# Routing matrices of every third batch made from two one-pass products, with GpSimd making part of the columns

## The reference, cut to what matters

```
e = (take_along_axis(i1, ci // 16) * 128 + take_along_axis(i2, ci % 16))
g = softmax(sc)                       # 16 shares for each of 8 heads
ue, ve = u[e], v[e]
hid = einsum('thkd,td->thk', ue, xb)
a = gelu(hid) * g
out = einsum('thk,thkd->td', a, ve)
```

## Time and profile before

| | |
|---|---|
| median of 3 runs | 3039.03 us (3038.13 to 3039.24) |
| span of the profiled execution | 3036.8 us |
| TensorE busy | 3010.5 us |
| VectorE, ScalarE, GpSimd busy | 1840.3, 1147.8, 1919.7 us |
| stage of the routing matrices | some 2242 to 2465 us |

### The profile page before, as it was taken

One profiled execution on the slowest core, in us unless ns is written; L12 is line 12 of the kernel. 1 busy time (PEld: TensorE's weight loads), 2 busy tenths in 40 slices (PEclk: granted clock), 3 DMA queues, 4 the chain that ended last, 5 costly groups with the idle time before them and its releaser, 6 DMA issues.

```text
span 3036.8 us, 42976 instructions
## 1 busy us (share of the span) xinstructions
PE 3010.5 (99%) x15307; PEld 2554.4 (84%) x15307; DVE 1840.3 (61%) x3382; ACT 1147.8 (38%) x2083; POOL 1919.7 (63%) x1812
## 2 busy tenths in 40 slices
PE   8999999999999999999999999999999999999999
PEld 7877888888668888888777888999999998888887
DVE  7675544316865442250673236888868859877785
ACT  3466222103652221120554212444367753333333
POOL 7423766677337666776433576798975576766763
PEclk9999999999999999999999999999999999999999
DMA  7211222223212222222112223699989999999995
GB/s 240 70 43 42 92 97 98 97 96 104 77 45 102 99 97 96 97 104 97 70 56 77 77 91 114 231 330 313 334 301 329 329 363 382 379 362 362 359 368 193
DMA packets 175167, 547.67 MB, mean 180 GB/s; under 512 B 13667, under 2 KB 67076, under 8 KB 155140
## 3 DMA queue, kind: packets, MB, share of 16 engines
q1 hardware_dynamic: 117348, 338.81, 32.5%
q0 software_dynamic: 39168, 142.62, 12.4%
q10 hardware_dynamic: 18464, 63.70, 5.7%
HBM read 487.55 MB, written 57.40 MB: 179 GB/s over the span
## 4 chain that ended last, share of the span: by engine, by line
PE 94%; ACT 2%; DVE 2%; POOL 1%; issue 1%; ACTq 0%; DMA 0%; DVEq 0%; POOLq 0%
PE banks L194 83%; PE banks L2974 2%; PE banks L2290 1%; PE banks L2251 1%; POOL weights_split L3552 1%; PE banks L1151 1%; PE banks L2269 1%; PE banks L2895 1%; PE banks L1807 1%; PE banks L1845 0%; PE banks L1220 0%; PE banks L1823 0%; PE banks L1210 0%; PE banks L1241 0%; DVE memory L3234 0%
## 5 line engine op out<-in xcount | busy, mean ns | idle before, releaser
L194 PE MATMUL banks<-memory,weights_split 128*128 128x512 f32 (+1 forms) x9456 | 2043.1, 373 | 9.6 <-DVE memory L578 8.3
L194 PEld LDWEIGHTS banks<-memory,weights_split 128*128 128x128 f32 x9456 | 1693.0, 188 | 279.1 <-issue 33.0
L3717 POOL TENSOR_SCALAR weights_split<-weights_raw 128x512 fp32r<-128x512 f32 x576 | 374.2, 659 | 748.9 <-issue 372.0
L3722 POOL TENSOR_TENSOR weights_split<-weights_raw,weights_split 128x512 fp32r<-128x512 f32 x576 | 767.6, 1344 | 0.2
L3552 POOL TENSOR_TENSOR weights_split<-weights_raw,weights_split 128x512 fp32r<-128x512 f32 x384 | 506.9, 1344 | 275.3 <-ACT weights_split L3351 272.9
L194 PE MATMUL banks<-weights_split,memory 128*128 128x512 f32 (+1 forms) x2880 | 646.4, 386 | 0.0
L194 PEld LDWEIGHTS banks<-weights_split,memory 128*128 128x128 f32 x2880 | 533.7, 188 | 108.9 <-issue 1.0
L3351 ACT ACTIVATE weights_split<-weights_raw 128x1024 fp32r<-128x1024 f32 x256 | 268.6, 1051 | 38.6 <-DMA weights_raw<-in_weights 20.7
L3054 DVE CUSTOM_DVE_ANT_0 memory<-memory,banks 128x1024 f32<-128x1024 f32 x144 | 174.2, 1213 | 71.4 <-DMA memory<-in_peer_u,memory 68.9
L712 DVE TENSOR_TENSOR banks<-banks,memory 128x512 f32<-128x512 f32 x88 | 61.3, 699 | 231.9 <-PE banks L194 231.8
L3546 POOL DMA_INDIRECT memory<-in_peer_v,memory x128 | 160.4, 1253 | 42.0 <-issue 25.9
(11 more groups left out here) (309 smaller groups left out, 2683.5 us busy)
## 6 DMA issues: line engine op xcount, KB each, us to landing
weights_raw<-in_weights SPq DMA_DIRECT2D x143, 1024.0 KB
weights_raw<-in_weights SPq DMA_DIRECT2D x257, 512.0 KB
routing<-memory ACTq DMA_DIRECT2D x12, 2048.0 KB
hidden<-memory ACTq DMA_DIRECT2D x62, 384.0 KB
memory<-hidden SPq DMA_DIRECT2D x31, 768.0 KB
memory<-routing SPq DMA_DIRECT2D x30, 768.0 KB
window_rows<-memory ACTq DMA_DIRECT2D x1, 3064.0 KB, 26.5
chunk_rows<-memory ACTq DMA_DIRECT2D x1, 2556.0 KB, 12.3
```

The source lines that it names most:

```text
L194: last = k.nc.tensor.matmul(out, left[a], right[b], start=start and n == 0, stop=stop and n == 2, skip_group_check=True)
L3717: k.nc.gpsimd.tensor_scalar(cut(high, n * PIECE, PIECE), cut(raw, n * PIECE, PIECE), 1.0, 1.0, ALU.mult, ALU.mult).then_inc(k.high_made, 1)
L3722: k.nc.gpsimd.tensor_tensor(cut(low, n * PIECE, PIECE), cut(raw, n * PIECE, PIECE), cut(high, n * PIECE, PIECE).bitcast(F32), ALU.subtract ...
```

## The change

For every third batch (g % 3 = 2) the shares no longer scale the rows. The share is split in two parts of type F32R, `share_high` (ScalarE, rounded) and `share_low` (VectorE, what is left). VectorE's `one_hot` writes such a batch as F32R, and `weigh_columns` scales its columns with the high part, in place of `weigh_rows`. GpSimd makes the columns of the lower part in `lower_columns(g)`: one instruction for each token compares the key numbers 0 to 127 with the choice's column and multiplies with the low share. TensorE then makes two one-pass products for each token, with the same rows, summed in PSUM, and writes each token's matrix contiguously; `copy_matrix` reads such a bank in the other order. The shares of these batches alone are copied to PSUM. Several semaphores are merged or renamed. The other two batches in three are as before.

```diff
+    with k.scope(at=8 * KB):
+        share_both, first_columns, second_columns = (k.take(512, F32R) for _ in range(3))
+        share_high, share_low = cut(share_both, 0, P), cut(share_both, P, P)
+        columns_low = [first_columns, second_columns]
+    with k.scope(at=exact_at):
+        exact_hots = [k.take(2 * BATCH * P, F32R) for _ in range(DEPTH)]
...
+    def exact_number(g):
+        return g // 3
...
-                pe.wait_ge(weighted, sum(not by_scalar(n) for n in range(g + 1)))
+                pe.wait_ge(weighted, exact_number(g) + 1)
+                pe.wait_ge(columns_lowered, BATCH * (exact_number(g) + 1))
...
             for t in range(BATCH):
-                last = mm(by_key[:, t, :], cut(hots[g % DEPTH], t * P, P), cut(hots[g % DEPTH], (BATCH + t) * P, P),
-                          start=True, stop=True, skip_group_check=True)
+                if by_scalar(g):
+                    last = mm(by_key[:, t, :], cut(hots[g % DEPTH], t * P, P), cut(hots[g % DEPTH], (BATCH + t) * P, P),
+                              start=True, stop=True, skip_group_check=True)
+                    continue
+                rows = cut(exact_hots[g % DEPTH], t * P, P)
+                out = cut(score_banks[g % 2].memory, t * P, P)
+                mm(out, rows, cut(exact_hots[g % DEPTH], (BATCH + t) * P, P), start=True, stop=False,
+                   skip_group_check=True)
+                last = mm(out, rows, cut(columns_low[exact_number(g) % 2], t * P, P), start=False, stop=True,
+                          skip_group_check=True)
...
-        def weigh_rows(g):
-            rows = cut(hots[g % DEPTH], 0, BATCH * P).rearrange("p (t n) -> p t n", t=BATCH)
+        def weigh_columns(g):
+            columns = cut(exact_hots[g % DEPTH], BATCH * P, BATCH * P).rearrange("p (t n) -> p t n", t=BATCH)
             dve.wait_ge(hot, g + 1)
-            v.tensor_tensor(rows, rows, cut(shares, g * BATCH, BATCH).unsqueeze(2).broadcast_to(three),
+            v.tensor_tensor(columns, columns.bitcast(F32),
+                            cut(shares, exact_number(g) * BATCH, BATCH).unsqueeze(2).broadcast_to(three),
                             ALU.mult).then_inc(weighted, 1)
...
-        dve.wait_ge(iota_placed, 2)
+        dve.wait_ge(matrix_inputs, 3)
+        v.tensor_tensor(share_low.rearrange("p (c n) -> p c n", n=BATCH), exact_shares,
+                        share_high.rearrange("p (c n) -> p c n", n=BATCH).bitcast(F32),
+                        ALU.subtract).then_inc(matrix_inputs, 1)
...
                          score_banks[g % 2].memory.rearrange("p (n t) -> p n t", t=BATCH),
+                         score_banks[g % 2].memory.rearrange(
+                             "p (n t) -> p n t" if by_scalar(g) else "p (t n) -> p n t", t=BATCH),
...
-                        a.activation(shares, cut(turned, 2 * DENSE, DENSE), ACT.Copy).then_inc(iota_placed, 1)
+                        a.activation(share_high.rearrange("p (c n) -> p c n", n=BATCH), exact_shares,
+                                     ACT.Copy).then_inc(matrix_inputs, 1)
+                        act.wait_ge(matrix_inputs, 2)
+                        a.activation(shares, share_high.bitcast(F32), ACT.Copy).then_inc(matrix_inputs, 1)
...
+        def lower_columns(g):
+            number = exact_number(g)
+            if number == 0:
+                pool.wait_ge(matrix_inputs, 4)
+            if number >= 2:
+                pool.wait_ge(made, g - 5)
+            k.hold(pool)
+            for t in range(BATCH):
+                k.nc.gpsimd.tensor_scalar(cut(columns_low[number % 2], t * P, P), k.const("iota"),
+                                          cut(turned, DENSE + g * BATCH + t, 1),
+                                          cut(share_low, number * BATCH + t, 1).bitcast(F32), ALU.is_equal,
+                                          ALU.mult).then_inc(columns_lowered, 1)
+
         for unit in range(UNITS):
+            for g in matrix_after.get(unit - 3, ()):
+                if not by_scalar(g):
+                    lower_columns(g)
             if not by_vector(unit):
                 pool.wait_ge(unit_high, unit + 1)
```

More of the change, by code:

```diff
@@ L2669, in expert_layer @@
         hots = [k.take(2 * BATCH * P) for _ in range(DEPTH)]
+        exact_at = k.pointer - DEPTH * 8 * BATCH * P
         expert_f, expert, share_of, hid, applied = (k.take(P) for _ in range(5))
@@ L2748, in expert_layer @@
     (keys_in, normalised, scored, copied, order, exp_in, exp_out, chosen_ready, turned_up, emptied, activated, hot,
-     weighted, made, matrix_copied, iota_placed, multiplied, high_made, ready, used, out_filled, gain_in, result_summed,
+     weighted, columns_lowered, made, matrix_copied, matrix_inputs, multiplied, high_made, ready, used, out_filled, gain_in, result_summed,
      result_sized, result_rooted, result_inverted, result_made, unit_begun, unit_high, residual_turned, residual_kept,
@@ L2752, in expert_layer @@
          "keys_in", "normalised", "scored", "scores_copied", "order", "to_exp", "exped", "chosen", "turned", "emptied",
-         "activated", "hot", "weighted", "made", "matrix_copied", "iota_placed", "multiplied", "high_made", "ready",
+         "activated", "hot", "weighted", "columns_lowered", "made", "matrix_copied", "matrix_inputs", "multiplied", "high_made", "ready",
          "used", "out_filled", "gain_in", "result_summed", "result_sized", "result_rooted", "result_inverted",
@@ L2758, in expert_layer @@
         k.lasting("experts_last_" + s) for s in ("weighed", "made", "scaled", "half_out"))
-    (ones_placed, picked_summed, masks_made, numbered, spread_copied, numbers_made, picked_turned,
+    (ones_placed, picked_summed, picking_made, spread_copied, numbers_made, picked_turned,
      factors_made, factors_placed, factors_turned, picked_weighed) = (k.lasting("experts_" + s) for s in (
-         "ones_placed", "picked_summed", "masks_made", "numbered", "spread_copied", "numbers_made", "picked_turned",
+         "ones_placed", "picked_summed", "picking_made", "spread_copied", "numbers_made", "picked_turned",
          "factors_made", "factors_placed", "factors_turned", "picked_weighed"))
@@ L2781, in expert_layer @@
     largest, inverse = cut(iota, 0, PEER_HEADS), cut(best_cols, 0, PEER_HEADS)
-    shares = cut(scratch_bank.memory, 0, DENSE)
+    shares = cut(scratch_bank.memory, 0, P)
+    exact_shares = cut(turned, 2 * DENSE, DENSE).rearrange("p (c n) -> p c n", n=3 * BATCH)[:, :, 2 * BATCH:3 * BATCH]
     index4 = index_f.rearrange("p (s h r) -> p h s r", h=PEER_HEADS, s=2)
@@ L2937, in spread_numbers @@
         def spread_numbers():
-            pe.wait_ge(masks_made, 3)
-            pe.wait_ge(numbered, 1)
+            pe.wait_ge(picking_made, 4)
             mm(score_banks[0].memory[:, 3 * P:4 * P], chooser, all_numbers, start=True,
@@ L3090, in make_masks @@
             ident = k.const("ident")
-            v.tensor_copy(by_group(chooser), repeated(ident[:, FIRST_PICKED:P])).then_inc(masks_made, 1)
-            v.tensor_reduce(group_mask, by_group(ident), AX.X, ALU.add).then_inc(masks_made, 1)
-            v.tensor_reduce(token_mask, ident.rearrange("p (q t) -> p t q", t=PICKED), AX.X, ALU.add).then_inc(masks_made, 1)
+            v.tensor_copy(by_group(chooser), repeated(ident[:, FIRST_PICKED:P])).then_inc(picking_made, 1)
+            v.tensor_reduce(group_mask, by_group(ident), AX.X, ALU.add).then_inc(picking_made, 1)
+            v.tensor_reduce(token_mask, ident.rearrange("p (q t) -> p t q", t=PICKED), AX.X, ALU.add).then_inc(picking_made, 1)
         def of_group(x):
@@ L3099, in take_numbers @@
             dve.wait_ge(spread_copied, 1)
-            dve.wait_ge(masks_made, 3)
+            dve.wait_ge(picking_made, 3)
             v.tensor_tensor(by_group(spread), by_group(spread), of_group(group_mask), ALU.mult).then_inc(numbers_made, 1)
@@ L3218, in route @@
                 v.scalar_tensor_tensor(out=all_numbers, in0=chosen[:, 0:P], scalar=float(PEER_KEYS), in1=chosen[:, P:2 * P],
-                                       op0=ALU.mult, op1=ALU.add).then_inc(numbered, 1)
+                                       op0=ALU.mult, op1=ALU.add).then_inc(picking_made, 1)
             consume(left[0])
@@ L3233, in one_hot @@
             both = [P, 2, BATCH, P]
-            v.tensor_tensor(hots[g % DEPTH].rearrange("p (s t n) -> p s t n", s=2, t=BATCH),
+            out = (hots if by_scalar(g) else exact_hots)[g % DEPTH]
+            v.tensor_tensor(out.rearrange("p (s t n) -> p s t n", s=2, t=BATCH),
                             iota.unsqueeze(1).unsqueeze(1).broadcast_to(both),
@@ L3297, in vector @@
             if not by_scalar(g):
-                weigh_rows(g)
+                weigh_columns(g)
         consume(BEFORE_GATES)
@@ L3394, in copy_matrix @@
             a.activation(by_key[:, :, at:at + BATCH],
-                         score_banks[g % 2].memory.rearrange("p (n t) -> p n t", t=BATCH),
+                         score_banks[g % 2].memory.rearrange(
```

(8 more changed lines are left out.)

## The result

The changed kernel takes 3304.63 us (median of 5 runs, 3303.64 to 3306.20), the kernel before in the same rounds 3038.13 us (3037.43 to 3039.24). The ratio is 1.0877 (95% interval 1.0865 to 1.0889): 266 us, or 8.8%, slower. The forecast was 3227 us, slower, with a range of 3120 to 3320. Sign, place and mechanism were right. The size was 78 us short.

A forecast was written before the change was run, and what follows sets the result against it. The prediction took TensorE's own work to bound the kernel (3010.5 of 3036.8 us busy). Adding 158 us for the ring and 30 for the clock gave a span of 3224.8 us; the median, 2.2 higher, was 3227, range 3120 to 3320.

The forecast's parts named there:

- Sign, place and mechanism: Slower (0.89), in the stage of the routing matrices, by TensorE waiting for GpSimd's late columns in a ring (0.80).
- TensorE gains nothing: Exact batches on TensorE: eight one-pass records, paced by the weight load, take the old 0.93 us; gain 0.
- The bounds of -13 and +30 us: TensorE's 32 exact batches: 13 us less if the moving side sets the pace, 30 more at double price.
- The columns are late by their place: GpSimd's queue: columns begin only after unit n + 2's low part and fetches, late in every unit by 3 us or more.
- the stage becomes a ring: Routing-matrix stage: copies wait for batches, so split and GpSimd wait for TensorE, which waits for GpSimd; +158 us.
- The rival of columns that come in time: GpSimd delivers without lateness: 3037 to 3041 (0.05), 3026 (0.06) or 3069 (0.03), by the products' pace.
- The rival of the shorter ring: GpSimd's fetches and columns fall into its waiting time, not behind the low part: +67, 3106; chance 0.06.
- The ring's sum: Steps from exact batch to columns: 10.89, 11.82 or 12.75 us per turn by position; stage 383.3 against 225.1 us.
- the price of a column instruction: GpSimd's 128x128 instruction: 0.27 us, 1.08 a batch, from a line between two other rows; bounds 0.10 and 0.66.
- The clock: TensorE idles 4 to 6 us per ring, so its clock likely falls: half of 60 us taken, +30 us.
- VectorE and ScalarE cost nothing: One-hot stays 1.22 us, weighing columns 0.68, new work under 1 us once; reordered bank copy taken as 0.
- What the profile would show: TensorE's waits name GpSimd's columns 32 times, some 150 us; busy about 94%; units of 11 to 13 us.

The follow-up runs named there:

- the kernel with the products alone: Changed kernel without GpSimd's low columns; TensorE's second product of each token reads the high columns again: 3037.89 us, 1.0000 to the kernel before.
- experiment 6: Changed kernel, but each GpSimd column instruction makes 16 of 128 columns and the second product moves 16: 3249.63 us, 1.0693 to the kernel before.
- ninth: Changed kernel with GpSimd's columns made two turns earlier and only 16 of 128 columns per instruction: 3037.97 us, 1.0000 to the kernel before.
- experiment 1: Changed kernel with GpSimd's columns made two turns earlier (unit - 1 in place of unit - 3): 3057.84 us, 1.0063 to the kernel before.
- experiment 3: Changed kernel with GpSimd's columns made ahead of the turn's gathers, right behind the low part: 3243.43 us, 1.0674 to the kernel before.
- (5): Changed kernel with GpSimd making each batch's four columns twice, TensorE waiting for the second set: 3409.44 us, 1.1223 to the kernel before.
- experiment 10: Changed kernel with the constant 1.0 in place of the low share in GpSimd's column instruction: 3294.53 us, one run.
- the filler kernel: Changed kernel with 20 extra one-pass products of 512 columns on TensorE ahead of each wait for the columns: 3271.66 us, 1.0769 to the kernel before.
- experiment 8: Changed kernel with GpSimd's columns made one turn earlier (unit - 2 at the top of the turn): 3061.39 us, 1.0077 to the kernel before.

## Why the prediction was right, and where it was short

*TensorE gains nothing.* Right. The record count of the stage is unchanged (1561), the pace of short one-pass records is 0.11 us, and the kernel with the products alone is at 1.0000. The bounds of -13 and +30 us are both excluded. The sixth and ninth experiments bear on the cause: with only 16 columns moved in every second record, the 8 records still go at the pace of 128 (1.70 us at the low clock, 2301.53 to 2303.23 in the sixth; 0.22 to 0.23 us for two records at full clock in the ninth). Moving fewer columns bought nothing while each record loaded 128 columns of weights.

*The columns are late by their place, and the stage becomes a ring.* Right, and shown from several sides: one digit moves 247 us (experiment 1), reordering with equal work moves 61 (3), doubling the columns adds 105 (5). The rival of columns that come in time needed GpSimd's busy share to count. It doesn't: GpSimd was free for 93 of 223 us before the change, and in the changed kernel it idles for 254 of 488, waiting for the very split that TensorE's batches hold up. The rival of the shorter ring is excluded by the turn in the timeline, where gather and columns stand behind the low part, and by experiment 3: with the gathers out of the ring the kernel is 61 us faster, so they had been in it.

*The ring's sum.* Right but for two terms. The forecast for a turn like the one shown (exact batch first, one scaled batch in the next unit, one gather) is 12.75 - 1.17 - 0.53 = 11.05 us; it took 15.38 (2307.04 to 2322.42). The steps from copy to gather hold within 0.1 us each: 0.50, 1.17, 1.23, 2.67, against 0.50, 1.17, 1.23, 2.64. The gather takes 1.08, against 1.24. What differs is the columns, 3.13 against 1.08, and the three batches up to the start of the last copy, 5.49 us (2307.04 to 2312.53) against 2.99. That is 2.05 and 2.50 us; less some 0.2 for the gather and the hand-over, it is the 4.3. The other turns agree: between the first and the last exact batch lie 31, and in them the gathers take 1.78 us on average (forecast 1.77) and the columns 3.13.

*The term that was sized wrong is the price of a column instruction*, "With two scalar operands I take 0.27". It is 0.786 us, above the upper bound of 0.66 as well. The line between a 512-column row and a one-column memset was drawn through two other forms. Neither reads an operand per partition, and this one has a high fixed part (some 370 ns by experiment 6); with a constant in place of the share per partition the instruction takes 75 ns less (experiment 10). 32 x (3.13 - 1.08) = 66 us of the missing 78. That the result still lies in the range is in part luck: with the columns at 0.786 and the full price of the clock the sum would have been 3036.8 + 158 + 66 + 60 + 2.2 = 3323.

*The clock.* Right that it falls, but half of the full price was taken, 30 us of 60, and it was more. What is left of 266 after 158 and 66 is 42. The trace has it directly: the step from the start of an exact batch to the start of its unit's last copy takes 1.94 us on average where one batch is in it (10 turns), 3.80 with two (12) and 5.25 with three (8), against 1.13, 2.06 and 2.99 in the forecast. That is 47 us over 30 turns (the 31st holds a unit without an exact batch). In the filler kernel the same sum is 17 us, with every other step of the turn as long as before within 0.1 us, but for the hand-over in three turns (up to 0.8 us more), at a clock of 0.94 instead of 0.74; these 30 us are nearly all of the 33 that it gains. 66 and 17 too little make 83 against the missing 78; the other 5 us lie in smaller terms that weren't taken apart. How the clock stands within the turn, by stretch, from the columns to the next ones:

```profile
2300.00:2307.00 7.00, 0.00 (x0) 0.00 (x0) 0.00 (x0) 0.48 (x1) 6.65 (x7) 0.66 0.39 126
2307.00:2309.00 2.00, 1.96 (x9) 2.00 (x10) 0.00 (x0) 0.00 (x0) 0.00 (x0) 0.50 0.20 82
2309.00:2312.50 3.50, 3.50 (x17) 3.50 (x18) 3.49 (x5) 1.19 (x2) 0.00 (x0) 0.50 0.00 0
2312.50:2316.50 4.00, 4.00 (x24) 3.75 (x23) 2.97 (x5) 2.71 (x6) 1.07 (x1) 1.00 0.00 0
```

TensorE idles for 7 us, in which the clock falls from 2.4 to 1.2 GHz (by single microseconds it is 1.00 until 2302 and 0.50 from 2303 on). The exact batch and those behind it run at the low level, and they are the ones in the ring. In this turn the hidden unit gets the high level back, where it is worth nothing; in the next one it runs at 0.50 until 2329, and costs nothing either, since the columns come later still. This is the pattern that the Trainium skill ("TensorE: Matmul & The Clock Gate", HAM oscillation) describes for bursts with long waits between; the trace agrees. The forecast's reason for taking half, that shorter waits fall less surely, did not hold for waits of this size: the idle in front of L2991 was 5.7 us on average, within the forecast's 4 to 6, and in experiment 3, with 4.0 us on average (129 us in 32), the clock of the stage still stood at 0.76 and the same sum over the batches at 44 us. With the waits of experiment 8, at most 1.8 us, it stood at 0.99.

*VectorE and ScalarE cost nothing.* Right: the F32R one-hot takes 1.22 us, weighing the columns 0.68, and the copy of a bank in the other order 0.60 us for all 96 (minimum 597, maximum 600 ns).

*What the profile would show.* TensorE's waits were to name GpSimd's columns 32 times, with some 150 us in all. There are 32 waits, with 184 us, but the changed kernel's profile names the columns for 9 of them (37.6 us) and puts 22 down to "issue"; the filler kernel's names them 29 times. For the others the releaser had to be read from the timeline. TensorE's share fell to 94% as forecast. The turns with an exact batch took 12.7 to 18.3 us (the one with a further unit inside 22.0), not 11 to 13.

## What to carry to other kernels

A free engine is no free place: before work goes to an engine with idle time, look up what it waits for there, and whether the consumer of the new work is upstream of that wait. If it is, every us of the engine's turn joins the critical path, whatever its busy share; where the queue offers an earlier turn, the same work costs its load alone. And count the weight loads of short products before splitting one into cheaper passes: here, with 128 columns moved or fewer, as many loads took as much time.

## What was not expected of the hardware

A GpSimd comparison and multiplication with two per-partition operands takes 786 ns for 128 columns, more than the mean of 659 ns of a 128x512 instruction with constants; 711 ns with one of the operands constant, 420 ns for 16 columns. A one-pass record of 128 columns starts every 0.11 us at full clock and every 0.215 us at the 1.2 GHz level (2307.28, 2307.49 and 2307.71 in the changed kernel's timeline), and the record of the weight load lengthens with it, from 192 to 333 ns. With 16 columns moved in every second record two records still take 0.43 us at that level (2302.38 to 2302.81), though the single starts lie 0.25 and 0.18 us apart:

```profile
2302.38 0.45 PE L2991 MATMUL banks<-memory 128*128 128x128 f32 x1
...
2302.63 0.32 PE L2993 MATMUL banks<-memory,memory 128*128 128x16 f32 x1
...
2302.81 0.45 PE L2991 MATMUL banks<-memory 128*128 128x128 f32 x1
```
